# Expert gate and up weights read in runs of 8 KB, token rows stored in the matching column order

## The chip, the cores and the metric

The kernel runs on one core of a Trainium2 chip. The metric is the device time of one execution in microseconds (us). Five engines work side by side, each on its own instruction stream: TensorE (PE in the profile, with PEld for its weight loads), VectorE (DVE), ScalarE (ACT), GpSimd (POOL) and SyncE (SP). They wait for each other through semaphores only. Transfers between HBM and the on-chip memory go through DMA queues; SP and POOL issue those that matter here.

## The reference

The program is one layer of a streaming encoder: a mix of differential attention and gated DeltaNet, a cross attention, and a mixture of experts, for 512 prompt tokens and 8 x 16 sample tokens (640 tokens of 1024 columns). The change is in the last part:

```python
def rmsnorm(x, g):
    y = x * lax.rsqrt(jnp.mean(x * x, axis=-1, keepdims=True) + NORM_EPS)
    return y * g

def hier_moe(x, w_grp, b_grp, w_rt, b_rt, w_gate, w_up, w_down):   # x = rmsnorm(x, g_ffn), 640 x 1024
    grp_prob = softmax(x @ w_grp + b_grp)                 # 4 groups
    g_top, g_idx = top_k(grp_prob, 1)
    e_logits = (x @ w_rt + b_rt).reshape(N, 4, 8)         # 8 experts to a group
    in_grp = e_logits of the chosen group
    e_top, e_idx = top_k(in_grp, 2)
    e_w = softmax(e_top) * g_top
    ...
    for each expert e:   # w_gate, w_up: 32 x 1024 x 256, w_down: 32 x 256 x 1024, float32
        hg = silu(x @ w_gate[e]) * (x @ w_up[e])
        out = out + (hg * comb[:, e]) @ w_down[e]
    return out
```

Each token goes to two experts. The kernel computes only those pairs.

## The kernel before

Everything is float32. A token tile is 128 tokens; there are five (NT = 5, t = 0 to 4), four of the prompt and one of the samples. 1024 columns are KC = 8 chunks of P = 128.

**The norm ahead of the experts.** For each token tile ACT sums the squares (L313), POOL makes the reciprocal root in two small instructions (L321, L323), DVE multiplies the tile by it into one of two buffers `scr` (L336, in `norm_dve_rows`), PE transposes the eight chunks (L357), and DVE multiplies the transposed chunks by the gain (L343). These transposed tiles feed the router. PE's last product ahead of the norm is the cross attention's output; DVE adds it to x (L438).

**The rows that the experts gather.** In `ffn_rows_pool` POOL multiplies the same `scr` buffer by a row of gains that is spread over the partitions (L2015, 128 x 1024), and stores the tile in HBM as `h_rows` (L2017). POOL runs its instructions in the order in which they are written: norm 0, norm 1, product 0, store 0, norm 2, product 1, store 1, norm 3, product 2, store 2, norm 4, product 3, store 3, product 4, store 4. So POOL's part of the norm of tile t + 2 stands behind the product and the store of tile t. DVE's L336 for tile t waits for POOL's norm of t, and, since there are two buffers, for the product t - 2.

**The router.** PE, ACT and DVE compute the router's product (L1819, L1825), choose the experts and make a table: blocks of CAP = 80 token slots, each block of one expert. It is one chain of dependent small instructions, and the expert loop begins when it ends.

**The expert loop.** A block j uses buffer k = j modulo 2. SP loads its three weights of 1 MB each (`moe_sync`): gate and up (L2048) and down (L2051), each as soon as PE has finished with what the buffer held two blocks earlier. `W` has 6144 floats on each partition for each k: 2048 of gate, 2048 of up, 2048 of down. POOL gathers 80 rows of `h_rows` (L2069); PE transposes them into chunks (L2094), multiplies by gate and up (L2110), and by down (L2119); POOL scatters the 80 result rows to `pair_rows` in HBM (L2082). PE waits for all three weights at once (`s_ew[k]`) before a block. The loop runs over 16 rounds of two blocks.

Before the change row 128 c + p of gate and of up lies on partition p as chunk c. One partition's data therefore come from eight places of 256 floats (1 KB) in HBM. Down has two rows of 1024 floats (4 KB) to a partition, each from its own place.

Of the kernel before, what the change touches and what calls it, by code (L numbers as in the profile page):

```python
# [16 lines left out]
ALU = mybir.AluOpType  # L17
# [3 lines left out]
P = 128  # L21
D = 1024
KC = D // P
# [185 lines left out]
def build_encoder_step(nc, a):  # L209

    ctx = ExitStack()
    with ctx:
        def sb(name, shape, dt=F32):
            return ctx.enter_context(nc.sbuf_tensor("sb_" + name, shape, dt))

        def sem(name):
            return ctx.enter_context(nc.semaphore(name))
# [14 lines left out]
        scr = sb("scr", [P, 3, D])  # L232
# [82 lines left out]
        def norm_pool_tile(pool, k, t):  # L315
            s = n_pool[k]
            if t == 0:
                s.arm(pool)
            pool.wait_ge(n_act[k][f"sq{t}"], n_act[k].after(0, f"sq{t}"))
            c = slice(t, t + 1)  # L320
            nc.gpsimd.tensor_scalar(rstd[k][:, c], ssq[k][:, c], 1.0 / D, EPS, ALU.mult, ALU.add).then_inc(s.step(f"ms{t}"), 1)  # L321
            pool.wait_ge(s[f"ms{t}"], s.after(0, f"ms{t}"))
            nc.gpsimd.tensor_tensor(rstd[k][:, c], rstd[k][:, c], C("minus_half")[:, 0:1], ALU.pow).then_inc(s.step(f"rn{t}"), 1)  # L323
# [1431 lines left out]
        h_row = conv[:, 4 * D:6 * D].rearrange("p (t d) -> p t d", t=2)  # L1755
        gffn_row = conv[:, 6144:7168]
# [246 lines left out]
        def ffn_rows_pool(pool):  # L2003

            s = n_pool["ffn"]
            pool.wait_ge(s_route, 64)
            for u in range(NT + 1):
                if u < NT:
                    norm_pool_tile(pool, "ffn", u)
                if u >= 1:  # L2010
                    t = u - 1
                    pool.wait_ge(n_dve["ffn"][f"xn{t}"], n_dve["ffn"].after(0, f"xn{t}"))
                    if t >= 2:
                        pool.wait_ge(s_rows[t % 2], 16 * (t // 2))
                    nc.gpsimd.tensor_tensor(h_row[:, t % 2, :], scr[:, t % 2, :], gffn_row, ALU.mult).then_inc(s.step(f"g{t}"), 1)  # L2015
                    pool.wait_ge(s[f"g{t}"], s.after(0, f"g{t}"))
                    pool.dma_start(a["h_rows"][t * P:(t + 1) * P, :], h_row[:, t % 2, :]).then_inc(s_rows[t % 2], 16)  # L2017
            for k in range(2):
                pool.wait_ge(s_rows[k], H_ROWS[k])
# [9 lines left out]
        s_ew = [sem(f"expert_loaded{k}") for k in range(2)]  # L2029
# [4 lines left out]
        def rounds(eng):  # L2034
            eng.wait_ge(r_dve["tabn"], r_dve.after(0, "tabn"))
            return eng.value_load(table_u[0:1, 0:1], min_val=1, max_val=(BLKPAD + 1) // 2)

        def moe_sync(sp):
            def load(i, k):
                j = 2 * i + k if isinstance(i, int) else sp.snap(2 * i + k)  # L2040
                at = slice(j + 1, j + 2) if isinstance(i, int) else bass.ds(j + 1, 1)
                e = sp.value_load(table_u[0:1, at], min_val=0, max_val=NE - 1)
                if k == 1:
                    sp.wait_ge(s_xg[0], i * 16 + 16)
                w = W[:, k, :]
                for m, (name, step) in enumerate((("w_gate", "gate"), ("w_up", "up"))):
                    sp.wait_ge(e_pe[step], e_pe.after(j - 2, step))
                    sp.dma_start(w[:, 2048 * m:2048 * m + 2048].rearrange("p (c f) -> p c f", c=KC),  # L2048
                                 a[name][0][bass.ds(e, 1)].rearrange("o (c p) f -> p (o c) f", p=P)).then_inc(s_ew[k], 16)
                sp.wait_ge(e_pe["d1"], e_pe.after(j - 2, "d1"))  # L2050
                sp.dma_start(w[:, 4096:6144].rearrange("p (f d) -> p f d", f=2),  # L2051
                             a["w_down"][0][bass.ds(e, 1)].rearrange("o (f p) d -> p (o f) d", p=P)).then_inc(s_ew[k], 16)


            sp.wait_ge(r_dve["tab"], r_dve.after(0, "tab"))
            for k in range(2):
                load(0, k)
            n = rounds(sp)
            with sp.Fori(1, n) as i:
                for k in range(2):  # L2060
                    load(i, k)
# [419 lines left out]
        @block.gpsimd  # L2481
        def _(pool):
            prep_pool_a(pool)
            pool.wait_ge(s_ident, 16)
            for t in range(NT):
                norm_pool_tile(pool, "mix", t)
            da_pool(pool)
            gdn_pool(pool)
            for k in ("mem", "cross"):
                for t in range(NORMS[k]):  # L2490
                    norm_pool_tile(pool, k, t)
            ffn_rows_pool(pool)
            moe_pool(pool)
            final_pool(pool)
# [33 lines left out]
```

## Time and profile before

| | |
|---|---|
| runs | 1437.18 us median of 3 (1430.82 to 1438.62) |
| profiled execution | span 1429.8 us; no other time of it is given |
| PE busy | 1250.6 us (87%) |
| DVE, ACT, POOL busy | 435.8, 310.1, 193.1 us |
| DMA | 221.49 MB in 143148 packets, 93611 of them under 2 KB |
| gate, up, down | 32 transfers of 1024 KB each |

The span is the time from the first to the last instruction of one profiled execution. The expert loop fills the stretch from about 1018 to 1392 us of it, the norm and the router the stretch from about 946 to 1013 us. A row of the timeline gives the start in us, the duration in us, engine, line, operation and tiles; in brackets stands the idle time before it and what ended that. A row of a stretch gives for each engine the busy time in it, then the granted TensorE clock (1.00 is 2.4 GHz, 0.50 is 1.2 GHz), the mean busy share of the DMA engines and the rate in GB/s.

### The profile page before, as it was taken

The numbers are of one execution on the slowest core, as the hardware profiler recorded it, in microseconds if no ns is written. First come the engines' busy times: TensorE is split into PE (matmuls) and PEld (weight loads), VectorE is DVE, ScalarE is ACT, GpSimd is POOL, SyncE is SP. The second block draws the span as 40 slices with busy tenths as digits, with TensorE's granted clock in tenths as the row PEclk, the third lists the DMA queues.
The fourth block names the chain that finished last, engine by engine and source line by source line (L and its number), as shares of the span: only waits on it lengthen the run. The fifth ranks groups of instructions, "written<-read, shape, count | busy, mean of one in ns | idle before, by whom it ended". The sixth has DMA issues, their size and how long they took to land.

```text
span 1429.8 us, 18302 instructions
## 1 busy us (share of the span) xinstructions
PE 1250.6 (87%) x7028; PEld 838.9 (59%) x7028; DVE 435.8 (30%) x949; ACT 310.1 (22%) x620; POOL 193.1 (14%) x222
## 2 busy tenths in 40 slices
PE   5999999987788789989999859994599999999990
PEld 3544555446677676654455644442577778777770
DVE  2002223326656564443210313345211111111115
ACT  2000557524223222102000212220011111111111
POOL 1000454301001001001000000031011111111114
PEclk9999999997989999999999979997599999999995
DMA  8111103111211314007460044410799999999966
GB/s 247 59 59 59 42 18 133 60 48 40 94 60 59 117 59 148 0 0 257 151 221 0 1 176 176 177 45 31 241 293 337 334 338 342 329 335 331 339 199 239
DMA packets 143148, 221.49 MB, mean 155 GB/s; under 512 B 18987, under 2 KB 93611, under 8 KB 142974
## 3 DMA queue, kind: packets, MB, share of 16 engines
q1 hardware_dynamic: 134564, 191.20, 40.1%
q0 software_dynamic: 8496, 29.50, 6.1%
q8 instruction: 31, 0.51, 0.1%
q10 hardware_dynamic: 42, 0.17, 0.1%
q14 instruction: 15, 0.12, 0.0%
HBM read 197.87 MB, written 22.97 MB: 154 GB/s over the span
## 4 chain that ended last, share of the span: by engine, by line
PE 72%; issue 15%; DVE 7%; DMA 2%; ACT 2%; POOL 1%; SPq 1%; DVEq 0%; POOLq 0%; ACTq 0%
PE bank L415 17%; PE bank L2110 16%; PE bank L411 14%; PE bank L2119 8%; PE bank L1074 3%; PE bank L2094 1%; PE bank L1614 1%; PE bank L1684 1%; DMA sb_W<-cache_mem_v 1%; PE bank L721 1%; PE bank L1079 1%; PE bank L741 1%; PE bank L357 1%; PE bank L1587 1%; PE bank L406 1%
## 5 line engine op out<-in xcount | busy, mean ns | idle before, releaser
L2110 PEld LDWEIGHTS bank<-sb_act_b,sb_W 128*128 128x128 f32 x2048 | 240.1, 196 | 17.2 <-issue 17.2
L2110 PE MATMUL bank<-sb_act_b,sb_W 128*128 128x80 f32 x2048 | 239.2, 279 | 0.9 <-DVE sb_act_b L2151 0.9
L415 PE MATMUL bank<-sb_W,sb_act_a 128*128 128x512 f32 x480 | 219.1, 603 | 1.7 <-issue 1.0
L411 PE MATMUL bank<-sb_act_a,sb_W 128*128 128x512 f32 (+1 forms) x768 | 213.1, 435 | 1.3 <-DVE sb_act_a L343 1.3
L411 PEld LDWEIGHTS bank<-sb_act_a,sb_W 128*128 128x128 f32 x768 | 116.0, 191 | 92.8 <-issue 90.7
L415 PEld LDWEIGHTS bank<-sb_W,sb_act_a 128*128 128x128 f32 x480 | 88.8, 193 | 101.2 <-issue 99.6
L2119 PE MATMUL bank<-sb_W,sb_act_b 128*80 128x512 f32 x256 | 118.8, 607 | 1.1
L1074 PE MATMUL bank<-sb_x 128*128 128x128 f32 x512 | 68.3, 284 | 9.7 <-DVE sb_x L1463 6.2
L2164 DVE TENSOR_TENSOR sb_act_b<-bank,sb_act_b 128x160 f32<-128x160 f32 x32 | 10.4, 324 | 216.3 <-PE bank L2110 216.3
L2119 PEld LDWEIGHTS bank<-sb_W,sb_act_b 128*80 128x80 f32 x256 | 36.4, 152 | 60.8 <-issue 60.8
L1074 PEld LDWEIGHTS bank<-sb_x 128*128 128x128 f32 x512 | 61.9, 194 | 16.3 <-DVE sb_x L1463 6.5
L2082 POOL DMA_INDIRECT pair_rows<-sb_act_b,sb_attn x32 | 29.6, 926 | 306.1 <-DVE sb_act_b L2169 306.1
L415 PE MATMUL bank<-sb_W 128*128 128x512 f32 x128 | 56.0, 593 | 1.4 <-DVE sb_W L343 1.4
L2169 DVE COPY sb_act_b<-bank 80x512 f32<-80x512 f32 x32 | 22.0, 687 | 100.2 <-PE bank L2119 100.2
L2128 ACT COPY sb_act_b<-bank 128x320 f32<-128x320 f32 x33 | 14.1, 426 | 147.9 <-PE bank L2094 147.9
L440 ACT COPY sb_conv<-bank 128x512 f32<-128x512 f32 x24 | 14.1, 586 | 147.8 <-PE bank L415 123.8
L321 POOL TENSOR_SCALAR sb_small<-sb_small 128x1 f32<-128x1 f32 x17 | 3.9, 232 | 298.7 <-ACT sb_scr L313 298.4
L415 PEld LDWEIGHTS bank<-sb_W 128*128 128x128 f32 x128 | 23.8, 190 | 29.4 <-issue 27.7
L415 PE MATMUL bank<-sb_conv,sb_act_a 128*128 128x512 f32 x80 | 39.4, 603 | 0.0
L2069 POOL DMA_INDIRECT sb_act_a<-h_rows,sb_attn x34 | 30.8, 907 | 57.0 <-DVE sb_attn L2147 47.3
L2135 ACT ACTIVATE sb_act_b<-bank 128x160 f32<-128x160 f32 x32 | 9.7, 304 | 129.6 <-PE bank L2110 129.6
L357 PE MATMUL bank<-sb_const,sb_scr 128*128 128x128 f32 x136 | 19.8, 303 | 19.5 <-DVE sb_scr L336 19.5
(381 smaller groups left out, 1487.9 us busy)
## 6 DMA issues: line engine op xcount, KB each, us to landing
sb_W<-w_gate SPq DMA_DIRECT2D x32, 1024.0 KB
sb_W<-w_up SPq DMA_DIRECT2D x32, 1024.0 KB
sb_W<-w_down SPq DMA_DIRECT2D x32, 1024.0 KB
sb_W<-w_in SPq DMA_DIRECT2D x7, 2048.0 KB, 8.3
sb_W<-cache_diff_k SPq DMA_DIRECT2D x8, 1024.0 KB, 5.2
sb_W<-cache_diff_v SPq DMA_DIRECT2D x8, 1024.0 KB, 7.4
sb_W<-cache_mem_k SPq DMA_DIRECT2D x8, 1024.0 KB, 4.8
sb_W<-cache_mem_v SPq DMA_DIRECT2D x8, 1024.0 KB, 7.0
```

Of the source, the lines that this page charges most:

```text
L357: mm = nc.tensor.transpose(quarters(bank[4 + 2 * (t % 2) + i])[:, c, :], scr[:, t % 2, q * P:(q + 1) * P], ident)
L406: mm = nc.tensor.matmul(out[0:8, 0:cols.stop - cols.start], w_gab[:, c, :], src[:, c, cols], start=c == 0, stop=c == KC - 1)
L411: mm = nc.tensor.matmul(out[:, 0:cols.stop - cols.start], slot(unit)[:, c, m * P:(m + 1) * P], src[:, c, cols], start=c == 0, stop=c == KC ...
L415: mm = nc.tensor.matmul(out[:, :], src[:, c, ja * P:(ja + 1) * P], w, start=c == 0, stop=c == KC - 1)
L721: mm = nc.tensor.matmul(bank[2 + m][:, 0:P * (t + 1)], dq[rows, h, t * P:(t + 1) * P], dk[rows, h, 0:P * (t + 1)], start=True, stop=True)
L741: mm = nc.tensor.matmul(bank[6 + t % 2][:, h * P:(h + 1) * P], aT[q][:, k * P:(k + 1) * P], dv[:, k, h * P:(h + 1) * P], start=k == 0, sto ...
L1074: mm = nc.tensor.matmul(quarters(out)[:, h, :], h4(lhs)[:, h, :], h4(rhs)[:, h, :], start=start, stop=stop)
L2069: pool.indirect_dma_start(xg[k][0:CAP, :], None, a["h_rows"], bass.IndirectOffsetOnAxis(token_col[k][0:CAP, :], 0))\
L2082: pool.indirect_dma_start(a["pair_rows"], bass.IndirectOffsetOnAxis(pair_col[k][0:CAP, :], 0), yb[k][0:CAP, :], None)\
L2110: mm = nc.tensor.matmul(bank[2 + m][:, CAP * f:CAP * f + CAP], w[:, c, f * P:(f + 1) * P], xgT[k][:, c, :], start=c == 0, stop=c == KC - 1)
L2119: mm = nc.tensor.matmul(bank[4 + g][0:CAP, :], hT[k][:, f, :], w[:, f, 512 * g:512 * g + 512], start=f == 0, stop=f == 1)
L2169: nc.vector.tensor_copy(yb[k][0:CAP, 512:1024], bank[5][0:CAP, :]).then_inc(e_dve.step("y1"), 1)
```

## The change

Gate and up are read with another assignment of rows: partition p gets rows 8 p to 8 p + 7. These eight rows of 256 floats lie one behind the other in HBM, so a partition's data are one run of 8 KB. Chunk c on partition p is now row 8 p + c in place of row 128 c + p.

The product needs the token columns in the same order. So POOL's product writes its columns in another order: place 128 c + p of an `h_rows` row holds column 8 p + c. Its two inputs, `scr` and the row of gains, are now read with a step of 8 floats (32 bytes) from one element to the next; its output is written without gaps as before. The store, the gather, the transposes and the products are the same instructions. Each engine has the same instructions in the same order as before.

```diff
                     pool.wait_ge(n_dve["ffn"][f"xn{t}"], n_dve["ffn"].after(0, f"xn{t}"))
                     if t >= 2:
                         pool.wait_ge(s_rows[t % 2], 16 * (t // 2))
-                    nc.gpsimd.tensor_tensor(h_row[:, t % 2, :], scr[:, t % 2, :], gffn_row, ALU.mult).then_inc(s.step(f"g{t}"), 1)
+                    by_chunk = lambda v: v.rearrange("q (p c) -> q c p", c=KC)
+                    nc.gpsimd.tensor_tensor(h_row[:, t % 2, :].rearrange("q (c p) -> q c p", c=KC), by_chunk(scr[:, t % 2, :]),
+                                            by_chunk(gffn_row), ALU.mult).then_inc(s.step(f"g{t}"), 1)
...
                 for m, (name, step) in enumerate((("w_gate", "gate"), ("w_up", "up"))):
                     sp.wait_ge(e_pe[step], e_pe.after(j - 2, step))
-                    sp.dma_start(w[:, 2048 * m:2048 * m + 2048].rearrange("p (c f) -> p c f", c=KC),
-                                 a[name][0][bass.ds(e, 1)].rearrange("o (c p) f -> p (o c) f", p=P)).then_inc(s_ew[k], 16)
+                    sp.dma_start(w[:, 2048 * m:2048 * m + 2048],
+                                 a[name][0][bass.ds(e, 1)].rearrange("o (p c) f -> p (o c f)", c=KC)).then_inc(s_ew[k], 16)
```

## Rows read from the trace of the kernel before

**Rows 1.** The page: the span, and the granted TensorE clock in 40 slices.
```profile
span 1429.8 us, 18302 instructions
...
PEclk9999999997989999999999979997599999999995
```

**Rows 2.** Busy time in a stretch of the expert loop, with the columns' names.
```profile
core 0: us, PE busy (x) PEld busy (x) DVE busy (x) ACT busy (x) POOL busy (x), PEclk, DMA share, GB/s
1050.00:1300.00 250.00, 249.24 (x1762) 197.37 (x1761) 35.65 (x110) 43.09 (x78) 40.23 (x44) 1.00 1.04 334
```

**Rows 3.** Timeline of one block of the loop: the gate and up products, down's load.
```profile
1097.04 7.27 PE L2110 MATMUL bank<-sb_act_b,sb_W 128*128 128x80 f32 x64
...
1097.23 0.37 SPq L2051 DMA_DIRECT2D sb_W<-w_down  x1
...
1108.39 7.27 PE L2110 MATMUL bank<-sb_act_b,sb_W 128*128 128x80 f32 x64
```

**Rows 4.** Waits of SP's queue: line, releaser, total us, times, longest.
```profile
SPq L2048 <- PE bank L2110: 157.8, 60, 6.1
...
SPq L2051 <- PE bank L2119: 113.7, 30, 5.8
```

**Rows 5.** Two stretches of the first block's loads: gate and up, then down.
```profile
1002.00:1006.00 4.00, 0.00 (x0) 0.00 (x0) 3.83 (x7) 0.00 (x0) 0.00 (x0) 0.50 1.07 361
1007.00:1009.00 2.00, 2.00 (x17) 2.00 (x17) 0.00 (x0) 0.00 (x0) 0.00 (x0) 0.50 1.05 407
```

**Rows 6.** Timeline: the first gate load, and the first gather.
```profile
999.51 0.38 SPq L2048 DMA_DIRECT2D sb_W<-w_gate  x1
...
1013.69 1.00 POOL L2069 DMA_INDIRECT sb_act_a<-h_rows,sb_attn  x1 [42.50 <-DVE sb_attn L2147]
```

**Rows 7.** Timeline of POOL: products 1, 2, 3, norms 3, 4, the last store.
```profile
952.60 2.36 POOL L2015 TENSOR_TENSOR sb_conv<-sb_scr,sb_conv 128x1024 f32<-128x1024 f32 x1
...
956.26 0.57 POOL L323 TENSOR_TENSOR sb_small<-sb_small,sb_const 128x1 f32<-128x1 f32 x1
956.80 2.34 POOL L2015 TENSOR_TENSOR sb_conv<-sb_scr,sb_conv 128x1024 f32<-128x1024 f32 x1
...
964.10 0.56 POOL L323 TENSOR_TENSOR sb_small<-sb_small,sb_const 128x1 f32<-128x1 f32 x1
964.64 2.33 POOL L2015 TENSOR_TENSOR sb_conv<-sb_scr,sb_conv 128x1024 f32<-128x1024 f32 x1
...
970.59 0.60 POOL L2017 DMA_DIRECT2D h_rows<-sb_conv  x1 [0.30 <-POOL sb_conv L2015]
```

**Rows 8.** Timeline of DVE beside it: rows of tiles 2, 3, 4, and an addition.
```profile
955.05 0.74 DVE L336 TENSOR_SCALAR sb_scr<-sb_x,sb_small 128x1024 f32<-128x1024 f32 x1
...
956.91 2.79 DVE L336 TENSOR_SCALAR sb_scr<-sb_x,sb_small 128x1024 f32<-128x1024 f32 x1
961.86 0.69 DVE L438 TENSOR_TENSOR sb_x<-bank,sb_x 128x512 f32<-128x512 f32 x1 [2.17 <-PE bank L415]
...
964.70 2.83 DVE L336 TENSOR_SCALAR sb_scr<-sb_x,sb_small 128x1024 f32<-128x1024 f32 x1 [0.95 <-POOL sb_small L323]
```

**Rows 9.** POOL's groups by line: a sum of two 664-column inputs, a 1536-column copy.
```profile
L664 POOL TENSOR_TENSOR sb_scr<-sb_scr 128x664 f32<-128x664 f32 x12 | 19.3, 1606 | 0.0
...
L1324 POOL COPY sb_attn<-sb_conv 128x1536 f32 x2 | 2.9, 1464 | 17.8 <-PE bank L1130 17.8
```

**Rows 10.** Stretches around two idle gaps of PE, with the granted clock.
```profile
963.60:967.60 4.00, 0.02 (x1) 0.02 (x1) 3.05 (x3) 0.14 (x2) 3.38 (x4) 0.94 0.02 4
967.60:970.50 2.90, 2.90 (x10) 1.90 (x11) 2.54 (x5) 0.00 (x0) 2.67 (x2) 0.50 0.44 181
970.50:979.40 8.90, 8.55 (x37) 3.53 (x35) 0.00 (x0) 0.84 (x2) 0.60 (x1) 1.00 0.15 60
637.20:642.80 5.60, 0.13 (x1) 0.00 (x0) 4.12 (x7) 0.00 (x0) 1.01 (x1) 0.70 0.00 0
642.80:649.70 6.90, 6.18 (x10) 2.90 (x11) 2.40 (x3) 2.78 (x5) 1.71 (x4) 0.50 0.58 210
```

## The prediction

> **What bounds the kernel now.** I began with the page [rows 1]: the span is 1429.8 us, and the granted clock is high nearly throughout, with a hole before and at the start of the expert loop. Next I asked for the busy time in the middle of the loop, because the loads that change are there [rows 2]: PE is busy for 249.24 of 250.00 us at clock 1.00, while DMA moves 334 GB/s. So PE sets the pace. One block takes 1108.39 - 1097.04 = 11.35 us [rows 3]. The waits of SP say the same from the other side: gate and up loads stood 157.8 us behind PE's gate and up products, down loads 113.7 us behind PE's down products, 271.5 us in total [rows 4]. The buffers come free late; the data do not come late.
>
> Then I followed the chain of waits ahead of the loop, where the other half of the change stands. There POOL and DVE get in each other's way. DVE's L336 takes 0.74 us where POOL's product has just ended (tile 2), and 2.79 and 2.83 us where a product began just before it (tiles 3 and 4) [rows 7, 8]. The product of 964.64 ends at 966.97, L336 at 967.53: it ends 0.56 us after the product, as if it had been held until then. For tile 4 PE has nothing else to do: it is idle for 3.98 of the 4.00 us to 967.60 [rows 10]. So the duration of POOL's product is on the path that sets the end, although POOL is idle most of the time.
>
> **The loads.** Removed are short runs, 64 transfers of 1 MB (32 gate, 32 up) in runs of 1 KB; added are the same bytes in runs of 8 KB. No row has an 8 KB run. The nearest are in the first block, with nothing beside them: 361 GB/s while gate and up come in 1 KB runs, 407 GB/s while down comes in 4 KB runs [rows 5]. I take 407 for 8 KB: 2.10 MB then take 5.15 us in place of 5.81 us, 0.66 us less for a block, 21 us of transfer over 32 blocks. In the loop all of it lies beside PE. Down's load for a block is issued at 1097.23, and the block that uses its buffer next begins two blocks after its predecessor there, at 1108.39 [rows 3]: 11.16 us for a transfer of 2.6 us (1.05 MB at 407 GB/s). A load that ends sooner only lengthens that slack. Before the loop the first gate load is issued at 999.51; 8.4 us of transfers (5.81 + 2.6) and about 1.5 us until they flow end near 1009.5, and the first gather is issued only at 1013.69 [rows 6]. So the loads are worth 0 us. That cover would be gone only if the transfers of a block took over 11.35 us.
>
> **The product on POOL.** Five products read both inputs with a step of 32 bytes in place of 4. The row now is 2.34 us [rows 7]. From 664 to 1024 columns two-input instructions rise from 1.606 us [rows 9] to 2.34 us, or 2.04 ns a column, two reads and a write. A copy with one read takes 1464 / 1536 = 0.95 ns a column [rows 9]. No row shows a strided read of this size, so the bounds are: below, no price (2.34 us; less is excluded, since the same elements are read and written); above, every column costs twice as much, 2.34 + 1.024 x 2.04 = 4.43 us. Between them, one more read at the copy's price for one operand gives 2.34 + 0.98 = 3.3 us, and for both operands 4.3 us. I take the middle of these two, 3.8 us, the copy being the nearest row to one read more. So d = 1.45 us for each product (0 to 2.1).
>
> The Trainium skill (GPSIMD Engine Reference, section Performance pitfalls for Q7 kernels) speaks against the change here: a read from the on-chip memory with a step over 8 bytes costs about 2.9 cycles an element where a dense one costs 1.9, half as much again. By that alone the product would be an estimated 3.5 us and the final time about 1441 us; no run here shows it yet.
>
> What d does, in order of the engines' programs [rows 7, 8]:
> - Product 0 ends d later, and norm 2 behind it on POOL too. DVE wants L336 of tile 2 at 955.05, after norm 2; product 1 now ends at 954.96 + 2d = 957.9, and L336 is held until then: 2d late.
> - Norm 3 is 2d late and product 2, at once behind it, ends 3d later, at 959.14 + 3d. L336 of tile 3, now ending at 959.70, ends 3d later. DVE's next work, the last addition L438, begins at 961.86 after an idle 2.17 us [rows 8]. So of 3d = 4.35 us the first 2.17 are hidden, and 2.2 us reach the path. If that idle time were not there, all 4.35 would.
> - After L438 come ACT's squares, norm 4 on POOL, and product 3, which begins at the end of norm 4 and holds L336 of tile 4 as it does now: d more.
> - Product 4 and its store end 2.2 + 2d = 5.1 us later than now. Now the last store is issued at 970.59 and the first gather at 1013.69, behind the router [rows 6, 7]; 43 us hide it.
>
> Sum on the path: 1.45 + (4.35 - 2.17) = 3.6 us. The router is one chain, so all of this reaches the loop, whose blocks keep their 11.35 us.
>
> **The clock.** In the idle time ahead of tile 4 the granted clock falls to 0.50 and returns 2.9 us after PE resumes [rows 10]. This idle time now grows from 4.0 us to about 6.2 (part of the 3.6 us falls before tile 3's transposes). Another gap, of 5.6 us, was followed by 6.9 us at 0.50 [rows 10]. 4.0 us more at half speed cost 2.0 us of work at most; since the gap is not the same I take 1.5 us (0 to 2.0).
>
> Together 3.6 + 1.5 = 5.1 us: 1429.8 becomes 1434.9 us in the span. The span is 7.4 us under the median, 1437.18, and 1.0 under the fastest run; the runs lie 7.8 us apart, and I add to the median: 1442 us. With the bounds of d and the clock the two terms are 0 to 8.2 us (d = 2.1: 2.1 + 4.1 = 6.2, and 2.0), so the likeliest case's own range is 1438 to 1446.
>
> **Rivals.** First, a strided read has no price: the loads are hidden and the product is as before, 1437 us. For it: POOL's instructions may be held by their loop rather than by the reads. Against: at 2.04 ns for two reads and 0.95 for one, the time goes with the number of reads.
>
> Second, slower by more than can be called the same, by one mechanism at one place: POOL's product in front of L336. Each us of d costs 4 us less the hidden 2.17, so the path with the 1.5 us of the clock loses over 7.2 us from d = 1.95 on, a product of 4.3 us, the price of one more read for both operands. At the upper bound of d the path loses 6.2 us; the stretch of 8.90 us behind, with 8.55 us of PE work at clock 1.00 [rows 10], would lose up to 8.55 us if the clock stayed at 0.50 through it, half of which is 4.3. That is 1437.2 + 6.2 + 4.3 = 1448 us. For it: two operands are strided, not one. Against: the copy's price also holds a write.
>
> Third, the 8 KB transfers are slower than the old ones. Down needs 2.6 us a block, the 0.66 MB of gathers and scatters about 2.0 us at 334 GB/s; 6.8 us remain for 2.10 MB, so it decides below 308 GB/s. At 250 GB/s a block would take 13.0 us, 1.6 us more for 31 blocks, near 1487 us. Against: 407 beside 361 GB/s, the longer run being the faster.
>
> Fourth, the loads shorten the loop, because it waits for data in a way that the modelled ends of matmuls conceal. 3.8 MB at 407 GB/s are 9.3 us, 2.0 us less than now for 31 blocks: 1375 us. Against: SP's 271.5 us of waiting for PE.
>
> **How the numbers follow.** The forecast has 0.53, no price 0.17, the slow product 0.22, slower 8 KB transfers 0.03, the loop paced by data 0.02, and 0.03 are left for a median that lands low without a cause in the change. About 0.5%, 7.2 us, is what a measurement of this kernel can tell from no change: faster is under 1430.0, slower over 1444.4. Faster: 0.02 + 0.03, and 0.02 of the case without a price, 0.07. Slower: 0.22 + 0.03, and 0.03 of the forecast's upper end, 0.28. The same: 0.65. The range of 1433 to 1450 takes in the case without a price with a measurement some us under the median, and the slow product's 1448.
>
> **What would show it.** In the changed profile: PE still busy over 99% of the middle of the loop and a block still 11.35 us; SP waiting for PE at least 271 us; the DMA share in the loop lower at the same GB/s; POOL's product near 3.8 us, and L336 of tiles 2, 3 and 4 ending about 0.56 us after a product; L438's last instance with almost no idle time before it; the first gather 4 to 7 us later. A product still at 2.34 us, or L336 at 0.74 us beside it, would make the sum on POOL wrong; a shorter block would make the first part wrong.

## The result and the profile after

| | before | changed |
|---|---|---|
| median of 20 runs each | 1434.4 us (1430.45 to 1438.63) | 1439.81 us (1434.93 to 1444.24) |
| ratio, with its 95% interval | | 1.0034 (1.0021 to 1.0047) |
| span of the profiled execution | 1429.8 us | 1437.7 us |
| DMA packets | 143148 | 85804 |

The change costs 4.9 us by the ratio (3.0 to 6.7); the medians lie 5.4 us apart. That is clear of no change, and less than the 0.5% below which the prediction counts a time as the same. The profiled changed execution took 1439.55 us, 1.85 us more than its span. Two of the twelve executions of the changed kernel with a wait that is tried below, and one of the eleven of the kernel before with it, took between 2282 and 7232 us and are not in their ratios.

The loads first. These are the stretches that answer to [rows 5] and [rows 2] in the changed kernel: gate and up alone, then down alone in the first block, then the middle of the loop. The columns are those of [rows 2].

```profile
1011.00:1015.00 4.00, 0.00 (x0) 0.00 (x0) 3.83 (x6) 0.00 (x0) 0.00 (x0) 0.50 1.00 422
1016.00:1018.00 2.00, 1.96 (x15) 1.96 (x16) 0.00 (x0) 0.00 (x0) 0.00 (x0) 0.50 1.01 414
...
1050.00:1300.00 250.00, 249.24 (x1765) 197.62 (x1765) 35.63 (x110) 42.99 (x77) 40.13 (x44) 1.00 0.96 334
```

Gate and up now come at 422 GB/s where they came at 361, down at 414 beside 407. In the loop PE is busy for the same 249.24 of 250 us and DMA moves the same 334 GB/s, but its mean busy share is 0.96 where it was 1.04: the DMA engines need less time for the same bytes, and PE was not waiting for them. SP's waits show that too, beside [rows 4]; the columns are the same:

```profile
SPq L2050 <- PE bank L2112: 159.7, 60, 6.5
...
SPq L2053 <- PE bank L2121: 113.9, 30, 4.8
```

SP waits for PE 159.7 + 113.9 = 273.6 us in place of 271.5. A block takes 11.36 us, from the gate and up products at 1105.79 to the next at 1117.15, where it took 11.35.

Now POOL and DVE, beside [rows 7] and [rows 8]. First the changed kernel's timeline of POOL (start, duration, engine, line, operation):

```profile
958.48 3.87 POOL L2016 TENSOR_TENSOR sb_conv<-sb_scr,sb_conv 128x1024 f32<-128x1024 f32 x1
...
964.18 3.84 POOL L2016 TENSOR_TENSOR sb_conv<-sb_scr,sb_conv 128x1024 f32<-128x1024 f32 x1
...
971.26 3.77 POOL L2016 TENSOR_TENSOR sb_conv<-sb_scr,sb_conv 128x1024 f32<-128x1024 f32 x1
...
1023.25 1.00 POOL L2071 DMA_INDIRECT sb_act_a<-h_rows,sb_attn  x1 [42.51 <-DVE sb_attn L2149]
```

Then its DVE in the same stretch, from the addition (L438) that comes before tile 2's L336:

```profile
957.62 0.69 DVE L438 TENSOR_TENSOR sb_x<-bank,sb_x 128x512 f32<-128x512 f32 x1 [4.85 <-PE bank L415]
...
959.43 3.48 DVE L336 TENSOR_SCALAR sb_scr<-sb_x,sb_small 128x1024 f32<-128x1024 f32 x1
...
964.24 4.34 DVE L336 TENSOR_SCALAR sb_scr<-sb_x,sb_small 128x1024 f32<-128x1024 f32 x1
968.51 0.68 DVE L438 TENSOR_TENSOR sb_x<-bank,sb_x 128x512 f32<-128x512 f32 x1
...
971.32 4.27 DVE L336 TENSOR_SCALAR sb_scr<-sb_x,sb_small 128x1024 f32<-128x1024 f32 x1 [0.94 <-POOL sb_small L323]
```

Product 2 takes 3.84 us in place of 2.34, and L336 of tiles 2, 3 and 4 ends 0.56, 0.56 and 0.56 us after the product that was running (958.48 + 3.87 = 962.35 and 959.43 + 3.48 = 962.91, and so on). The last L438 has no bracket: its idle 2.17 us of before are gone. And these are PE's transposes of tile 4:

```profile
975.65 1.97 PE L357 MATMUL bank<-sb_const,sb_scr 128*128 128x128 f32 x8 [5.92 <-DVE sb_scr L336]
```

The two spans differ by 7.9 us, and most of it is not the change. The addition at 957.62 stood at 953.25 before: 4.4 us had been lost in stages that the change does not touch. A measure without that is the way from this addition to PE's transposes of tile 4. These are its two ends in the kernel before:

```profile
953.25 0.69 DVE L438 TENSOR_TENSOR sb_x<-bank,sb_x 128x512 f32<-128x512 f32 x1 [4.85 <-PE bank L415]
...
967.58 1.97 PE L357 MATMUL bank<-sb_const,sb_scr 128*128 128x128 f32 x8 [4.01 <-DVE sb_scr L336]
```

Before, the way is 967.58 - 953.25 = 14.33 us; now 975.65 - 957.62 = 18.03 us, 3.70 us more. I call it the way below.

### The profile page after: what moved, and what is told of

Read it like the earlier page. It is cut to its first block, busy times and chain, and to the rows that moved or that the text cites. A ratio compares the mean times of both kernels' runs of the same rounds, so it can differ in the third digit from the quotient of the medians.

```text
span 1437.7 us, 18302 instructions
## 1 busy us (share of the span) xinstructions
PE 1255.8 (87%) x7028; PEld 841.8 (59%) x7028; DVE 441.5 (31%) x949; ACT 310.1 (22%) x620; POOL 198.4 (14%) x222
## 2 busy tenths in 40 slices
DMA packets 85804, 221.49 MB, mean 154 GB/s; under 512 B 18987, under 2 KB 28075, under 8 KB 77438
## 4 chain that ended last, share of the span: by engine, by line
PE 71%; issue 15%; DVE 7%; DMA 2%; POOL 2%; ACT 2%; SPq 1%; DVEq 0%; POOLq 0%; ACTq 0%
PE bank L2112 16%; PE bank L415 16%; PE bank L411 14%; PE bank L2121 8%; PE bank L1074 3%; PE bank L2096 1%; PE bank L1614 1%; PE bank L1684 1%; DVE sb_scr L336 1%; DMA sb_W<-cache_mem_v 1%; PE bank L721 1%; PE bank L741 1%; PE bank L1079 1%; PE bank L1819 1%; PE bank L1587 1%
```

## The experiments

All ratios are to the kernel before, with their 95% intervals; one us is 0.0007 of the time. The theory is that the whole loss is POOL's product, through the L336 that it holds, and that the loads are hidden.

**Each half alone.** Either half by itself leaves out the matching of token columns and weight rows: the experts' numbers differ, the instructions and the bytes do not. The first kernel keeps the new loads and undoes the product:

```diff
-                    by_chunk = lambda v: v.rearrange("q (p c) -> q c p", c=KC)
-                    nc.gpsimd.tensor_tensor(h_row[:, t % 2, :].rearrange("q (c p) -> q c p", c=KC), by_chunk(scr[:, t % 2, :]),
-                                            by_chunk(gffn_row), ALU.mult).then_inc(s.step(f"g{t}"), 1)
+                    nc.gpsimd.tensor_tensor(h_row[:, t % 2, :], scr[:, t % 2, :], gffn_row, ALU.mult).then_inc(s.step(f"g{t}"), 1)
```

> Gate and up in 8 KB runs, POOL's product reading densely as before (so the token columns stay in the old order while the weight rows are in the new one). Theory (the loss is POOL's product, which holds DVE's L336; the loads are hidden behind PE): 0 us against the kernel before, within 2 us (ratio 0.999 to 1.001), block of the loop still 11.35 us, product 2.3 us. Rival A (the loss comes from the 8 KB transfers, the product is hidden): about 5 us slower, 1.0034. Rival B (the loads save time and the product costs more than what was measured): faster by some us, ratio under 0.998.

Measured: 1.0001 (0.9987 to 1.0016). Product 1 takes 2.36 us, the way is 973.51 - 959.18 = 14.33 us, PE is busy 249.23 of 250 us in the loop. The loads alone are worth nothing that can be told from 0.

The second keeps the new product and undoes the loads:

```diff
-                    sp.dma_start(w[:, 2048 * m:2048 * m + 2048],
-                                 a[name][0][bass.ds(e, 1)].rearrange("o (p c) f -> p (o c f)", c=KC)).then_inc(s_ew[k], 16)
+                    sp.dma_start(w[:, 2048 * m:2048 * m + 2048].rearrange("p (c f) -> p c f", c=KC),
+                                 a[name][0][bass.ds(e, 1)].rearrange("o (c p) f -> p (o c) f", p=P)).then_inc(s_ew[k], 16)
```

> The other half alone: POOL's product reads with a step of 8 floats, gate and up in 1 KB runs as before (again the two orders don't match). Theory: as the changed kernel, about 5 us slower than before (1.0034, 1.002 to 1.005), product 3.84 us, L336 of tiles 2, 3, 4 at 3.5 to 4.3 us. Rival A: no difference, 1.000. Rival B: more than 5 us slower, over 1.005.

Measured: 1.0041 (1.0024 to 1.0057). Product 1 takes 3.87 us, the way is 975.50 - 957.48 = 18.02 us. The product alone gives the whole loss. Rival A is out by both runs. Rival B is out by the loads alone, whose interval begins over 0.998; the interval of the product alone would still admit it.

**Take the hold on L336 away.** One wait on POOL puts product 3 behind L336 of tile 4, in the changed kernel and in the kernel before:

```diff
+                    if t == NT - 2:
+                        pool.wait_ge(n_dve["ffn"][f"xn{NT - 1}"], n_dve["ffn"].after(0, f"xn{NT - 1}"))
                     ... (the product of tile t)
```

> The changed kernel, with one wait added on POOL: product 3 waits until DVE has finished L336 of tile 4, so nothing holds that L336. Theory: L336 of tile 4 takes 0.74 us in place of 4.27, 3.5 us off the path; the 2.2 us that products 1 and 2 put ahead of L438 stay; with the clock the time is about that of the kernel before (ratio 0.999 to 1.001). Rival A (the product does not matter): as the changed kernel, 1.0034. Rival C (the wait that L336 loses is taken over by another, since product 3 then runs against the transposed tiles' DVE work): 1.002 or more.

Measured: 1.0015 (1.0001 to 1.0029).

> The kernel before with the same wait added on POOL. Theory: L336 of tile 4 takes 0.74 us in place of 2.83, 2.1 us off the path; PE's idle time ahead of tile 4 falls from 4.0 to 1.9 us, so the clock may stay at 1.00, up to 1.4 us more: 2 to 3.5 us faster (0.9975 to 0.9985). Rivals A and C: no difference, 1.000.

Measured: 0.9987 (0.9975 to 0.9999). Here is L336 of tile 4 and product 3 in the timeline of the kernel before with the wait:

```profile
969.54 0.75 DVE L336 TENSOR_SCALAR sb_scr<-sb_x,sb_small 128x1024 f32<-128x1024 f32 x1 [0.94 <-POOL sb_small L323]
...
970.46 2.35 POOL L2017 TENSOR_TENSOR sb_conv<-sb_scr,sb_conv 128x1024 f32<-128x1024 f32 x1 [0.96 <-DVE sb_scr L336]
```

L336 takes 0.75 us, with the product behind it and not beside it. So over 2 of its 2.83 us of before were a wait, and no semaphore made it: L336 had already begun. That the engines wait for each other through semaphores only, as the first section has it, holds for the start of an instruction; here one that was running was held by another engine's. The way is 970.35 - 958.09 = 12.26 us, 2.07 less, and the time agrees with -1.9 us (-3.6 to -0.1), a little short of the 2 to 3.5 us that I expected. PE's transposes of tile 4, now behind a gap of 1.93 us, take 1.09 us in place of 1.97: the clock stayed at 1.00 through them, as this expectation thought it might. In the changed kernel the way falls to 969.00 - 954.47 = 14.53 us, 0.2 more than before, by which the time should have been that of the kernel before; it was 2.2 us longer, with an interval that begins at 0.1. The rival that another wait takes its place (1.002 or more) lies inside that interval; the timeline does not show such a wait, and the remainder is taken up below.

**What part of the read is dear.** Only `scr` is read with the step. This leaves out the matching of the gains with their columns; the instructions are the same:

```diff
-                                            by_chunk(gffn_row), ALU.mult).then_inc(s.step(f"g{t}"), 1)
+                                            gffn_row.rearrange("q (c p) -> q c p", c=KC), ALU.mult).then_inc(s.step(f"g{t}"), 1)
```

> The changed kernel with only one input of POOL's product read with a step of 8 floats (scr); the row of gains is read densely, so the gains land on other columns than they belong to. It measures the price of one strided read. Theory (each strided operand costs the same): the product takes half of the added 1.5 us, 3.1 us; 3 x 0.75 = 2.25 us ahead of L438 are hidden by its 2.17, so about 0.8 us reach the path: 1.0005. Rival (one strided operand slows the whole loop over the columns as much as two): 3.84 us, 1.0034. Rival (only the second operand or the pair costs): 2.34 us, 1.000.

Measured: 1.0006 (0.9987 to 1.0025). Its row for product 2, and the idle time of DVE ahead of the last addition:

```profile
964.26 2.84 POOL L2016 TENSOR_TENSOR sb_conv<-sb_scr,sb_conv 128x1024 f32<-128x1024 f32 x1
```
```profile
968.33 0.69 DVE L438 TENSOR_TENSOR sb_x<-bank,sb_x 128x512 f32<-128x512 f32 x1 [0.68 <-PE bank L415]
```

The first strided operand costs 0.50 us, the second another 1.0: I had expected the same price for each, and neither that nor the rival, the whole price for one, is what came. The row of gains alone with the step was not tried. The time by itself cannot tell these cases apart; the rows can. The idle time ahead of L438 shows the arithmetic of the three products: 2.17 - 3 x 0.50 = 0.67, and the row has 0.68. The way is 14.84 us, 0.51 more than before, which is one product's delay alone.

The same result with dense reads and a strided write:

```diff
-                    by_chunk = lambda v: v.rearrange("q (p c) -> q c p", c=KC)
-                    ...
+                    rows_of = lambda v: v.rearrange("q (p c) -> q p c", c=KC)
+                    nc.gpsimd.tensor_tensor(h_row[:, t % 2, :].rearrange("q (c p) -> q p c", c=KC), rows_of(scr[:, t % 2, :]),
+                                            rows_of(gffn_row), ALU.mult).then_inc(s.step(f"g{t}"), 1)
```

> The changed kernel with the same result computed the other way round: both inputs of POOL's product read densely, the output written with a step of 128 floats (512 bytes). Theory (the price is in reads with a step): the product is back near 2.34 us, L336 at 0.74, 2.8 and 2.8 us as before the change, and the time is that of the kernel before: 1.000 (0.999 to 1.0015). Rival (a strided write costs as much or more): product 3.8 us or longer, 1.0034 or more.

Measured: 1.0000 (0.9984 to 1.0016). Product 2 in its timeline:

```profile
959.00 2.35 POOL L2016 TENSOR_TENSOR sb_conv<-sb_scr,sb_conv 128x1024 f32<-128x1024 f32 x1
```

2.35 us: writing with a step of 512 bytes costs nothing where reading with a step of 32 bytes cost 1.5 us. With the step on the write, the new loads cost nothing that these runs can tell from 0.

**The loads without cover.** SP starts a block's loads only when PE has finished the block ahead, in both kernels (shown here; the same for down):

```diff
-                    sp.wait_ge(e_pe[step], e_pe.after(j - 2, step))
+                    sp.wait_ge(e_pe["d1"], e_pe.after(j - 1, "d1"))
```

> The kernel before, with the cover of the loads taken away: SP starts a block's three loads only when PE has finished the block ahead, so PE waits for every load. Each block should take some 10 to 12 us longer, more where the clock falls in the idle time: 1434 + 32 x 10 to 32 x 20 us, 1750 to 2080 us. It is the reference for the next run.

Measured: 2140.71 us, 1.4904 (1.4866 to 1.4942). My forecast of 1750 to 2080 us was too low. The profile has 424.5 us in which PE waits for the loads, and 287.7 us more of busy time of PE than before, at a mean granted clock of 0.759; together about what was lost.

> The changed kernel with the cover taken away in the same way. Theory (8 KB runs are faster, and in the changed kernel hidden): the three loads of the first block took about 8.9 us before and 8.0 us after the change, so each of 32 blocks should be 0.7 to 0.9 us shorter than in the run with 1 KB runs: 22 to 29 us, less the 5 us of the product, 17 to 24 us under the run with 1 KB. Rival (8 KB runs are not faster where nothing runs beside them): same as the run with 1 KB plus 5 us.

Measured: 2098.27 us, 1.4614 (1.4577 to 1.4650): 42 us less. The waits of PE for the loads (total, times, longest), with 1 KB runs and with 8 KB runs:

```profile
PE bank L2110 <- DMA sb_W<-w_down: 424.5, 31, 14.3
```
```profile
PE bank L2112 <- DMA sb_W<-w_down: 400.3, 31, 13.3
```

24.2 us less in 31 waits, 0.78 us for a block, as the theory had it. The whole difference is larger than the 17 to 24 us that were expected, and PE's busy time says where: for the same products it is

```profile
PE 1538.3 (72%) x7028; PEld 1073.5 (50%) x7028; DVE 435.8 (20%) x949; ACT 310.1 (14%) x620; POOL 193.6 (9%) x222
```
```profile
PE 1517.2 (72%) x7028; PEld 1066.1 (51%) x7028; DVE 441.3 (21%) x949; ACT 310.1 (15%) x620; POOL 200.1 (10%) x222
```

21.1 us less, at a mean granted clock of 0.762 beside 0.759. I had priced the transfers and not the clock of the work between them; that the shorter idle time is what raised it was not tried by itself.

**Both repairs.** Strided write and the wait ahead of product 3 together:

> The changed kernel with both repairs: POOL reads densely and writes with the step, and product 3 waits until DVE has finished L336 of tile 4. Theory (the price is only in POOL's product and in the L336 that it holds): product 2.35 us, L336 of tile 4 0.75 us, and the time of the kernel before with the same wait, about 2 us faster than the kernel before (0.9987; 0.997 to 1.0). Rival (the loads in 8 KB runs cost something that the earlier runs hid in their spread): no better than the kernel before, 1.000 or more.

Measured: 0.9988 (0.9973 to 1.0004), 1431.63 us beside 1433.74. Product 2.36 us, L336 of tile 4 0.75 us, way 965.29 - 953.04 = 12.25 us. It agrees with the kernel before that has the wait alone; its interval just takes in no change, the other's just does not. The changed kernel's interval, 1.0021 to 1.0047, lies wholly above it. If it gains over the kernel before, the wait gives it and not the loads: the way is 12.26 us there with the old loads and 12.25 here.

## Why the prediction was right

1442 us was forecast and 1439.81 measured; as a difference 5.1 us were forecast and 4.9 measured (3.0 to 6.7). The mechanism and its sum were right. That the total came so close is in part luck: its last term, the clock, was not the change's, and the median of three runs that the forecast stood on, 1437.18 us, is 2.8 us above that of 20. Step by step:

- *The loads are worth 0 us.* Right: 1.0001 alone. 8 KB runs move at 422 GB/s, a little more than the 407 that I took, and without cover a block is 0.78 us shorter in its wait, where I had 0.66. The third and fourth rivals are out: the transfers are not slower, and the loop was not paced by data.
- *The product takes 3.8 us.* Right: 3.84. The middle between one more read for one operand and for both was a guess that hit; the run with one operand shows that the two reads do not cost the same. The first rival, no price, is out, and so is the second, which needed 4.3 us or more. The rule of the Trainium skill (GPSIMD Engine Reference, section Performance pitfalls for Q7 kernels), half as much again, gave an estimated 3.5 us. The measured factor is 3.84 / 2.34 = 1.64 for two strided operands and 2.85 / 2.34 = 1.22 for one: the sign agrees, the size does not.
- *L336 waits for the product to end.* Right: 0.56 us after it in each of three tiles, and 0.75 us when the product was moved. The Trainium skill (SBUF — State Buffer, section Who interferes with whom) has a reason: a VectorE instruction in a mode that uses both of its port pairs shares one with GpSimd, and whichever issues first holds that pair for its whole instruction while the other stops. It names operations of L336's kind (tensor_scalar) among those that can enter such a mode. The runs agree: 4.34 us for an L336 that begins 0.06 us after a product, 0.75 us with no product running. Which mode L336 was in, no row here shows.
- *3d, of which 2.17 us are hidden, and d again for tile 4: 3.6 us.* Right: the way is 3.70 us longer, and with the measured d, 1.50 us, the sum 4d - 2.17 is 3.8. The sign that the first gather would come 4 to 7 us later needs the addition as its zero: it is 9.6 us later in the spans and 5.2 counted from the addition.
- *The clock adds 1.5 us.* This term was mis-sized. I read from one execution that a gap of 4.0 us is followed by 2.9 us at 0.50 [rows 10], and that a longer gap would have more. In the profile with the loads alone the gap is the same 4.0 us, and these are the stretches after it there and in the changed kernel (gap 5.92 us):

```profile
969.50:973.50 4.00, 0.01 (x1) 0.00 (x0) 3.05 (x3) 0.17 (x2) 3.35 (x4) 0.92 0.00 0
973.50:979.90 6.40, 6.39 (x14) 2.61 (x15) 2.58 (x5) 0.00 (x0) 3.29 (x3) 0.52 0.41 168
```
```profile
975.65:981.60 5.95, 5.95 (x13) 2.49 (x14) 2.56 (x5) 0.00 (x0) 4.77 (x3) 0.50 0.28 113
```

  The clock stayed low for 6.4 us behind the shorter gap and for 5.95 behind the longer one. The run with the strided write and the one with bare loads in 1 KB runs, also with a gap of 4.0 us, have 6.4 us as well. So 2.9 us was the odd one of four, and the term should have been near 0. Beside the profile of before alone, the changed one has 5.95 - 2.9 = 3.05 us more at half speed, 1.5 us: the very number of the forecast, from a difference between executions that the change did not make.

- *The range.* From 1437.2 us, terms of 0 to 8.2 us reach from 1437.2 to 1445.4, where I wrote 1438 to 1446; nothing hangs on it.

Further along the path, the distance from the addition to the first gather takes in the whole router:

| profile | addition L438 | first gather | distance |
|---|---|---|---|
| before | 953.25 | 1013.69 | 60.44 |
| loads alone | 959.18 | 1021.19 | 62.01 |
| strided write | 955.43 | 1017.45 | 62.02 |
| changed | 957.62 | 1023.25 | 65.63 |
| product alone | 957.48 | 1023.05 | 65.57 |
| changed, with the wait | 954.47 | 1016.70 | 62.23 |
| before, with the wait | 958.09 | 1016.96 | 58.87 |
| both repairs | 953.04 | 1011.90 | 58.86 |

With dense reads it is 62.0 us, or 60.44 where the clock came back early; with the change's product it is 3.6 us more, whichever loads go with it. The two dense kernels with the wait need 3.1 us less than 62.0: 2.07 us are the hold, and about 1.1 go with the clock, whose stretch at 0.50 is about 3.4 us there (971.75 to 975.15 in the kernel before with the wait) in place of 6.4. From the addition to the end of the span it is 476.5 to 477.1 us in the first three profiles and 480.1 and 480.7 in the next two, so no further loss behind the addition is seen.

That leaves 3.0 to 4.2 us which the profiles show, about 3.6 by the first gather, and 4.9 us which the times show. The interval holds both. But the product alone (5.9 against 3.7) and the changed kernel with the wait (2.2 against 0.2) lie on the same side. Whether something else of one or two us comes with the slower product in the executions that were not profiled stays open.

## What to carry to other kernels

Read who waits for whom before pricing bytes: here SP waited 271 us for PE, and a sixth more speed of the loads was worth nothing until the prefetch was taken away. An engine that is idle 86% of the time can still be on the path, if another is held by its instructions: look for one instruction with two durations (0.74 and 2.8 us), and for what ran beside the long one. Where a layout must be permuted on POOL, try the step on the write: here it was free, and the step on the reads was not. And read a clock term from more than one profile.

## What the runs showed of the hardware

- POOL's product of two 1024-column float32 inputs: 2.35 us dense, 2.85 us with one input at a step of 32 bytes, 3.84 us with both, 2.36 us with dense inputs and an output at a step of 512 bytes (means of products 1 to 4; product 0, which begins while a dense L336 is still running, takes 2.78 us before and 4.29 us in the changed kernel).
- DVE's L336, alone 0.74 us, ends 0.56 us after a product that began before it, whether the product takes 2.34 or 3.84 us.
- The clock's return after a gap of PE is not fixed by the gap: 2.9 and 6.4 us behind two gaps of 4.0 us in different executions, 6.4 us behind one of 2.40 (the changed kernel with the wait), 5.95 us behind one of 5.92.
- The norm ahead of the experts began up to 6.7 us apart in profiles of kernels whose differences do not delay it (the addition L438 at 953.04 us with both repairs, at 959.71 with one strided operand). A difference of spans is no measure of a change of this size; a distance between two instructions around it is.
